# Gating projection's second half on 512-column matmuls in pairs of banks, and squares added ahead of three sums over partitions

## The chip, the cores and the metric

The kernel runs on one core of one Trainium2 chip. The metric is the device time of one execution in microseconds (us). The engines are named as in the profile: PE (TensorE, with PEld for its weight loads), DVE (VectorE), ACT (ScalarE), POOL (GpSimd), and SP, which here only issues DMAs.

## What is computed

The program is two residual blocks over 256 tokens of width 1024, one after the other, in fp32. Activations lie transposed on the chip: `x` is 128 partitions x 8 channel tiles x 256 tokens. What matters here, cut from the reference:

```python
def _spatial_gating_mixer(h, w_in, b_in, ln_g, ln_b, w_s, b_s, w_out):
    z = jax.nn.gelu(h @ w_in + b_in, approximate=False)
    u, v = jnp.split(z, 2, axis=-1)              # 2048 columns each
    v = _layernorm(v, ln_g, ln_b, LN_EPS)
    ...
    s = jnp.einsum('gij,bnjgc->bnigc', w_s, v) + b_s.T[None, None, :, :, None]
    y = u * s.reshape(bsz, seq, SGU_WIDTH)
    return y @ w_out

def _rmsnorm(x, g):
    y = xf * lax.rsqrt(jnp.mean(xf * xf, axis=-1, keepdims=True) + RMS_EPS)
    return (y * g.astype(jnp.float32)).astype(x.dtype)
```

The phases in order are a mixer, FFN 1, the gating mixer above, FFN 2, an RWKV mixer, FFN 3, and a last norm. Every norm needs the sum of the squares of a token over all 1024 channels, that is over 8 tiles and 128 partitions.

## The kernel before

Weights come in units of 128 x 2048 elements (1 MB) through a ring of four slots. For each unit SP loads `raw`, ACT rounds it to `w_high` (`high`, L685), DVE forms `w_low = raw - w_high` (`low`, L1264), and PE waits for the low part (`lo_done`). Activations are split in the same way, into `act_hi` and `act_lo`, which lie side by side in `act_parts`. A product is then hi x hi + hi x lo + lo x hi, accumulated in PSUM. Each engine's order is the order in which its own code is written; engines meet through semaphores.

There are two forms of that product. `split_matmul` (L2133 to L2135) issues three 256-column matmuls into one 256-column half of a bank; one unit (`project`) is 2 column tiles x 8 `k` x 3 matmuls in one bank. The FFNs use `wide` (L2496, L2497): one 512-column matmul takes `w_high` against both activation parts at once, so that the main term and the cross term land in the two halves of one bank, and a 256-column matmul adds `w_low` x `act_hi` to the second half. A unit then takes two banks, and the halves have to be added afterwards: ACT copies the second half to SBUF (`copy_half`, L897), DVE adds the first half from PSUM (`add_half`, L1584).

In the gating mixer (units 28 of the whole list onwards, `U_SGU`), eight units give `v` (banks 0 to 3), then eight units give `u`, one bank each, banks 0 and 1 in turn. For unit `c` of `u` the work is:

- PE: `project` after `u_raw >= c - 1` (the unit two before has left its bank); two `row_sums` ahead of `c` = 2, `spatial` ahead of `c` = 4 and 5. Before the first `accumulate` of the output projection, which writes banks 2 to 5, it waits for `v_raw >= 8`, the last use of banks 2 and 3.
- DVE: multiply the bank by the token scale `r2` (L1780, gives `u_raw`); from `c` = 1 on `low` of unit 11 + c; besides `normalise_values` at `c` = 1 (L1755), `row_sums` at 2 and 3 (L1713), two `final_norm` at 2 to 5 (L1718), and `gate(0)`, `gate(1)` at 5 and 6 (L1766, L1771, then L1775 after ACT's `gated_high`, L975).
- ACT: two Gelus after `u_raw` (L980), `high` of unit 12 + c, at `c` = 1 a table load and a small rsqrt (L697, L689, L691), at 5 and 6 `gated_high`.

Sums over partitions are fp32 matmuls against a matrix of ones. In the FFNs POOL first adds the eight tiles of squares (`fold_squares`, L637, L639) and PE needs one matmul (L2547). At the entry of the RWKV mixer PE takes eight (`input_sums`, L2650), tiles 0 to 5 in one row directly after FFN 2, tiles 6 and 7 after a first group of `small_products`. Ahead of the last norm it takes eight again (L3053), directly behind the last FFN matmul; ACT makes these squares (L1247 to L1251) as the tiles of `x` are finished, and DVE meanwhile finishes the last two tiles (`last_taken`, L1646 and L1648), multiplies `x` by the norm's weights (L2121) and at the end by the token scale (L2126). In `mlp(2)` ACT squares all of `x` for FFN 3's own norm in one instruction (L881) between the `high` of its third unit and that of its fourth.

## Time and profile before

| | |
|---|---|
| median of 3 runs | 1044.14 us (1043.94 to 1044.15) |
| profiled execution, its own time | 1044.1 us |
| its span, first to last instruction | 1042.2 us |
| PE busy | 1025.3 us, 98% |
| DVE busy | 824.7 us, 79% |
| ACT busy | 558.9 us, 54% |
| POOL busy | 54.9 us, 5% |
| mean granted TensorE clock | 0.998 |

In a row of the timeline the first number is the start in us from the start of the span, the second the duration. A matmul's record includes the time in which it fills and drains, so records overlap: the pace of PE is the distance from start to start, not the duration. The span is 1.9 us shorter than the execution's own time; that part lies around the program.

### The profile page before, as it was taken

Reading aid. Unit: us, or ns where it says so; the run is one execution under the profiler, and the core shown is the slowest. Engines: PE = TensorE matmul, PEld = TensorE weight load, DVE = VectorE, ACT = ScalarE, POOL = GpSimd, SP = SyncE. Lnnn points to the kernel's source line nnn. Section 1 sums busy time; section 2 is a strip of 40 time slices with the busy share of each in tenths; the row PEclk is TensorE's granted clock in tenths of the full one; section 3 lists DMA queues with packets and bytes.
Section 4 is the critical chain, followed back from the end, with each engine's and each line's share of the span. In section 5 each row is a group of like instructions: output and inputs, shape, how many; then the busy total and the mean of one; then the engine's idle time right before and its main releaser. Section 6 shows DMA issues by size and latency. Waiting matters only on the chain.

```text
span 1042.2 us, 17910 instructions
## 1 busy us (share of the span) xinstructions
PE 1025.3 (98%) x7496; PEld 927.8 (89%) x7496; DVE 824.7 (79%) x1167; ACT 558.9 (54%) x685; POOL 54.9 (5%) x48
## 2 busy tenths in 40 slices
PE   7999999999999999999999999999999999999997
PEld 7999988888887899998888889999898998888886
DVE  6989688677787787678878878899978668877775
ACT  6847554544456464355446447797543255444441
POOL 0004030000000000020000000042000001000000
PEclk9999999999999999999999999999999999999999
DMA  9722566566846745555656555424100156656621
GB/s 291 230 82 82 162 202 202 162 204 187 311 147 184 221 162 205 160 168 166 199 174 222 166 199 162 142 86 150 50 3 2 52 185 210 202 163 201 191 93 41
DMA packets 155937, 167.24 MB, mean 160 GB/s; under 512 B 5840, under 2 KB 148816, under 8 KB 155472
## 3 DMA queue, kind: packets, MB, share of 16 engines
q1 hardware_dynamic: 154672, 165.92, 50.2%
q8 instruction: 60, 0.98, 0.4%
q10 hardware_dynamic: 1184, 0.17, 0.2%
q14 instruction: 21, 0.17, 0.0%
HBM read 165.03 MB, written 1.05 MB: 159 GB/s over the span
## 4 chain that ended last, share of the span: by engine, by line
PE 83%; DVE 11%; ACT 3%; issue 2%; SPq 1%; DMA 1%; DVEq 0%; ACTq 0%
PE banks L2496 32%; PE banks L2497 16%; PE banks L2133 8%; PE banks L2135 8%; PE banks L2134 8%; DVE sb_w_low L1264 2%; DVE sb_arena L1966 1%; DVE sb_state L1963 1%; DMA sb_raw<-in_w_in 1%; ACT sb_w_high L685 1%; PE banks L2754 1%; PE banks L2621 1%; SPq L550 1%; PE banks L2865 0%; DVE sb_arena L1432 0%
## 5 line engine op out<-in xcount | busy, mean ns | idle before, releaser
L1264 DVE TENSOR_TENSOR sb_w_low<-sb_raw,sb_w_high 128x2048 fp32r<-128x2048 f32 x148 | 341.3, 2310 | 33.1 <-ACT sb_w_high L685 33.1
L685 ACT ACTIVATE sb_w_high<-sb_raw 128x2048 fp32r<-128x2048 f32 x148 | 281.7, 1908 | 11.3 <-PE banks L2135 10.2
L2496 PE MATMUL banks<-sb_act_parts,sb_w_high 128*128 128x512 f32 x768 | 270.6, 394 | 0.4 <-DVE sb_act_parts L1529 0.4
L2497 PE MATMUL banks<-sb_act_parts,sb_w_low 128*128 128x256 f32 x768 | 214.5, 279 | 0.0
L897 ACT ACTIVATE sb_arena<-banks 128x512 f32<-128x512 f32 x93 | 55.5, 597 | 244.7 <-PE banks L2497 244.7
L2496 PEld LDWEIGHTS banks<-sb_act_parts,sb_w_high 128*128 128x128 f32 x768 | 143.9, 187 | 36.1 <-DVE sb_act_parts L1529 0.7
L2133 PE MATMUL banks<-sb_act_parts,sb_w_low 128*128 128x256 f32 x584 | 169.3, 290 | 0.7 <-DVE sb_arena L1839 0.7
L2135 PE MATMUL banks<-sb_act_parts,sb_w_high 128*128 128x256 f32 x584 | 165.0, 282 | 0.0
L2134 PE MATMUL banks<-sb_act_parts,sb_w_high 128*128 128x256 f32 x584 | 163.9, 281 | 0.0
L2497 PEld LDWEIGHTS banks<-sb_act_parts,sb_w_low 128*128 128x128 f32 x768 | 144.0, 188 | 0.0
L2496 PE MATMUL banks<-sb_hidden_slots,sb_w_high 128*128 128x512 f32 x360 | 131.5, 397 | 0.6 <-DVE sb_hidden_slot L1597 0.6
L1584 DVE TENSOR_TENSOR sb_arena<-sb_arena,banks 128x512 f32<-128x512 f32 x93 | 63.7, 685 | 86.1 <-ACT sb_arena L897 86.0
L2496 PE MATMUL banks<-sb_hidden_slot,sb_w_high 128*128 128x512 f32 x360 | 130.2, 394 | 0.0
L2133 PEld LDWEIGHTS banks<-sb_act_parts,sb_w_low 128*128 128x128 f32 x584 | 109.9, 188 | 2.5 <-DVE sb_arena L1839 0.9
L2134 PEld LDWEIGHTS banks<-sb_act_parts,sb_w_high 128*128 128x128 f32 x584 | 110.8, 190 | 0.5 <-issue 0.2
L2135 PEld LDWEIGHTS banks<-sb_act_parts,sb_w_high 128*128 128x128 f32 x584 | 109.3, 187 | 0.0
L2497 PE MATMUL banks<-sb_hidden_slots,sb_w_low 128*128 128x256 f32 x360 | 101.1, 281 | 0.0
L2497 PE MATMUL banks<-sb_hidden_slot,sb_w_low 128*128 128x256 f32 x360 | 100.8, 280 | 0.0
L2496 PEld LDWEIGHTS banks<-sb_hidden_slots,sb_w_high 128*128 128x128 f32 x360 | 67.7, 188 | 17.5 <-DVE sb_w_low L1264 0.9
L2496 PEld LDWEIGHTS banks<-sb_hidden_slot,sb_w_high 128*128 128x128 f32 x360 | 67.5, 187 | 16.1
L2497 PEld LDWEIGHTS banks<-sb_hidden_slots,sb_w_low 128*128 128x128 f32 x360 | 67.6, 188 | 0.1
L2497 PEld LDWEIGHTS banks<-sb_hidden_slot,sb_w_low 128*128 128x128 f32 x360 | 67.5, 188 | 0.0
(473 smaller groups left out, 1544.2 us busy)
## 6 DMA issues: line engine op xcount, KB each, us to landing
sb_raw<-in_ffn_w SPq DMA_DIRECT2D x64, 1024.0 KB, 5.4
sb_raw<-in_w_up SPq DMA_DIRECT2D x16, 1024.0 KB, 5.5
sb_raw<-in_w_down SPq DMA_DIRECT2D x16, 1024.0 KB, 5.1
sb_raw<-in_sgu_w_in SPq DMA_DIRECT2D x16, 1024.0 KB, 5.6
sb_raw<-in_rwkv_w_rkv SPq DMA_DIRECT2D x12, 1024.0 KB, 5.2
sb_raw<-in_w_in SPq DMA_DIRECT2D x8, 1024.0 KB, 9.7
sb_raw<-in_sgu_w_out SPq DMA_DIRECT2D x8, 1024.0 KB, 4.9
sb_raw<-in_w_out SPq DMA_DIRECT2D x4, 1024.0 KB, 5.2
```

Of the source, the lines that this page charges most:

```text
L550: sp.dma_start(half_of(raw[j], t), w_in_v[:, :, c * 256 + t * P:c * 256 + t * P + P])\
L685: nc.scalar.activation(whi[s][:], raw[s][:], ACT.Copy).then_inc(hi_done, 1)
L897: nc.scalar.activation(dst, halves_at(FFN_BANK(m))[:, :, 1, :], ACT.Copy).then_inc(half_copied, 1)
L1264: nc.vector.tensor_tensor(wlo[s][:], raw[s][:], f32(whi[s][:]), ALU.subtract).then_inc(lo_done, 1)
L1584: nc.vector.tensor_tensor(t, t, halves_at(FFN_BANK(m))[:, :, 0, :], ALU.add).then_inc(unit_taken, 1)
L1963: base.add(nc.vector.tensor_tensor(tmp, RW.LB[:, j + 1:, j:j + 1].broadcast_to(shape), RW.WB[:, j:j + 1, 0:j + 1].broadcast_to(shape), ALU ...
L1966: base.add(nc.vector.tensor_tensor(RW.WB[:, j + 1:, 0:j + 1], RW.WB[:, j + 1:, 0:j + 1], tmp, ALU.add))
L2133: nc.tensor.matmul(dst, l_lo, r_hi, start=start, stop=False, **kw)
L2134: nc.tensor.matmul(dst, l_hi, r_lo, start=False, stop=False, **kw)
L2135: return nc.tensor.matmul(dst, l_hi, r_hi, start=False, stop=stop, **kw)
L2496: nc.tensor.matmul(two(dst), l_hi, parts, start=start, stop=False, skip_group_check=True)
L2497: return nc.tensor.matmul(dst[:, T:2 * T], l_lo, parts[:, 0, :], start=False, stop=stop, skip_group_check=True)
```

## The change

The eight `u` units of the gating mixer are issued with `wide`, into two banks each (0, 1 and 2, 3 in turn). ACT copies the second halves, DVE adds the first ones and then multiplies by `r2` in SBUF. PE now waits for the DVE addition (`u_added`), also ahead of the first `accumulate`. At the RWKV entry POOL adds the squares of tiles 0 to 3, so that PE takes one matmul for them. Ahead of the last norm POOL adds tiles 0 to 3 to two, DVE adds tiles 4 and 5 to those and both to one, in the middle of `last_taken`, and PE takes three matmuls. In FFN 3 the large square on ACT moves behind `high` of the fourth unit and the first `copy_half`.

```diff
@@ block.gpsimd, on["rwkv"] @@
+            pool.wait_ge(sq_done, SQ["rwkv"] + 2)
+            chain.add(pool.tensor_tensor(RW.sq[:, 0:2, :], RW.sq[:, 0:2, :], RW.sq[:, 2:4, :], ALU.add))
+            chain.settle()
+            pool.tensor_tensor(RW.sq[:, 0, :], RW.sq[:, 0, :], RW.sq[:, 1, :], ALU.add).then_inc(sq_paired, 1)
@@ block.gpsimd, on["end"] @@
             fold_squares(2)
+            pool.wait_ge(sq_done, SQ["final"] + 2)
+            pool.tensor_tensor(FB.sq[:, 0:2, :], FB.sq[:, 0:2, :], FB.sq[:, 2:4, :], ALU.add).then_inc(sq_paired, 1)
@@ block.scalar, mlp @@
-            nc.scalar.activation(FB.sq[:], x[:], ACT.Square).then_inc(sq_done, 1)
+            if j < 2:
+                nc.scalar.activation(FB.sq[:], x[:], ACT.Square).then_inc(sq_done, 1)
             high(u0 + 3)
...
                 copy_half(m)
+                if j == 2 and m == 0:
+                    nc.scalar.activation(FB.sq[:], x[:], ACT.Square).then_inc(sq_done, 1)
@@ block.scalar, gating, for c in range(8) @@
+                act.wait_ge(w_used, U_SGU + 8 + c + 1)
+                nc.scalar.activation(SG.U[:, 2 * c:2 * c + 2, :], halves_at(2 * (c % 2))[:, :, 1, :], ACT.Copy)\
+                    .then_inc(u_half, 1)
                 act.wait_ge(u_raw, c + 1)
@@ block.vector, mlp @@
+            def gather_squares():
+                dve.wait_ge(sq_paired, 2)
+                dve.wait_ge(sq_done, SQ["final"] + 3)
+                chain.add(nc.vector.tensor_tensor(FB.sq[:, 0:2, :], FB.sq[:, 0:2, :], FB.sq[:, 4:6, :], ALU.add))
+                chain.settle()
+                nc.vector.tensor_tensor(FB.sq[:, 0, :], FB.sq[:, 0, :], FB.sq[:, 1, :], ALU.add).then_inc(sq_gathered, 1)
...
                     if i:
+                        if j == 2:
+                            gather_squares()
                         dve.wait_ge(w_used, u0 + len(FFN_ORDER))
@@ block.vector, gating, for c in range(8) @@
-                dve.wait_ge(w_used, U_SGU + 8 + c + 1)
-                nc.vector.tensor_tensor(SG.U[:, 2 * c:2 * c + 2, :], two(bank[c % 2][:]), over(r2, 2), ALU.mult)\
-                    .then_inc(u_raw, 1)
+                us = SG.U[:, 2 * c:2 * c + 2, :]
+                dve.wait_ge(u_half, c + 1)
+                nc.vector.tensor_tensor(us, us, halves_at(2 * (c % 2))[:, :, 0, :], ALU.add).then_inc(u_added, 1)
+                dve.wait_ge(u_added, c + 1)
+                nc.vector.tensor_tensor(us, us, over(r2, 2), ALU.mult).then_inc(u_raw, 1)
@@ block.tensor @@
+        def project_wide(u, b):
...
+            for t in range(2):
+                for k in range(KT):
+                    cs = slice(t * P, t * P + P)
+                    ins = wide(bank[b + t], h[:, k, cs], l[:, k, cs], act_parts[:, :, k, :], start=k == 0,
+                               stop=k == KT - 1)
+            ins.then_inc(w_used, 1)
@@ gating, for c in range(8) @@
                 if c >= 2:
-                    pe.wait_ge(u_raw, c - 1)
+                    pe.wait_ge(u_added, c - 1)
                 else:
-                    pe.wait_ge(v_raw, 6)
-                project(U_SGU + 8 + c, c % 2)
-            pe.wait_ge(v_raw, 8)
+                    pe.wait_ge(v_raw, 6 + 2 * c)
+                project_wide(U_SGU + 8 + c, 2 * (c % 2))
+            pe.wait_ge(u_added, 8)
             pe.wait_ge(t_done, 4)
@@ input_sums @@
-                pe.wait_ge(sq_done, SQ["rwkv"] + c + 1)
-                for k in (2 * c, 2 * c + 1):
+                if c == 0:
+                    pe.wait_ge(sq_paired, 1)
+                else:
+                    pe.wait_ge(sq_done, SQ["rwkv"] + c + 1)
+                for k in (2 * c, 2 * c + 1) if c else (0,):
@@ on["end"] @@
-            for k in range(KT):
-                pe.wait_ge(sq_done, SQ["final"] + (k // 2 + 1 if k < 6 else k - 2))
-                ins = nc.tensor.matmul(bank[6][:, 0:T], ones, FB.sq[:, k, :], start=k == 0, stop=k == KT - 1)
+            pe.wait_ge(sq_gathered, 1)
+            nc.tensor.matmul(bank[6][:, 0:T], ones, FB.sq[:, 0, :], start=True, stop=False)
+            for k in (6, 7):
+                pe.wait_ge(sq_done, SQ["final"] + k - 2)
+                ins = nc.tensor.matmul(bank[6][:, 0:T], ones, FB.sq[:, k, :], start=False, stop=k == KT - 1)
```

ACT, end of the gating mixer's `u` loop, before: the Gelus and `high` of `c` = 5, `gated_high(0)`, then `c` = 6 with `gated_high(1)`, then `c` = 7. L685 is `high`, L975 `gated_high`, L980 a Gelu; in brackets the semaphores waited for.

```order
L980 ACTIVATE sb_arena<-sb_arena,sb_vectors 128x256
L685 ACTIVATE sb_w_high<-sb_raw 128x2048 [waits unit_used,unit_landed0]
L975 ACTIVATE sb_hidden_high<-sb_arena 128x512 [waits gated]
L980 ACTIVATE sb_arena<-sb_arena,sb_vectors 128x256 [waits u_in]
L980 ACTIVATE sb_arena<-sb_arena,sb_vectors 128x256
L685 ACTIVATE sb_w_high<-sb_raw 128x2048 [waits unit_used,unit_landed1]
```

The same place with the change, from `c` = 6 on: L692 is `high`, L985 `gated_high`, L989 the new copy of the second halves, L993 a Gelu.

```order
L989 ACTIVATE sb_arena<-banks 128x512 [waits unit_used]
L993 ACTIVATE sb_arena<-sb_arena,sb_vectors 128x256 [waits u_in]
L993 ACTIVATE sb_arena<-sb_arena,sb_vectors 128x256
L692 ACTIVATE sb_w_high<-sb_raw 128x2048 [waits unit_used,unit_landed0]
L985 ACTIVATE sb_hidden_high<-sb_arena 128x512 [waits gated]
L989 ACTIVATE sb_arena<-banks 128x512 [waits unit_used]
L993 ACTIVATE sb_arena<-sb_arena,sb_vectors 128x256 [waits u_in]
L993 ACTIVATE sb_arena<-sb_arena,sb_vectors 128x256
```

The copy of the last unit stands behind `high`, and behind a `gated_high` that waits for DVE.

DVE at the same place with the change, from `gate(0)` on: L1789 to L1798 are `gate`, L1804 is the new addition, L1806 the multiplication, L1277 is `low`.

```order
L1798 TENSOR_TENSOR sb_hidden_low<-sb_arena,sb_hidden_high 128x512 [waits gated,hidden_hi]
L1804 TENSOR_TENSOR sb_arena<-sb_arena,banks 128x512 [waits u_half_copied]
L1806 TENSOR_TENSOR sb_arena<-sb_arena 128x512 [waits u_halves_added]
L1277 TENSOR_TENSOR sb_w_low<-sb_raw,sb_w_high 128x2048 [waits unit_high]
L1789 SCALAR_TENSOR_TENSOR sb_arena<-banks,sb_vectors,sb_arena 128x256 [waits spatial_in_psum]
L1789 SCALAR_TENSOR_TENSOR sb_arena<-banks,sb_vectors,sb_arena 128x256
L1794 TENSOR_TENSOR sb_arena<-sb_arena 128x512 [waits u_activated,dve_chain]
L1798 TENSOR_TENSOR sb_hidden_low<-sb_arena,sb_hidden_high 128x512 [waits gated,hidden_hi]
L1804 TENSOR_TENSOR sb_arena<-sb_arena,banks 128x512 [waits u_half_copied]
L1806 TENSOR_TENSOR sb_arena<-sb_arena 128x512 [waits u_halves_added]
```

Each unit has two DVE instructions where it had one; the addition of the last unit stands behind `low` and all of `gate(1)`.

PE with the change, the last `wide` pair of the last `u` unit and the first matmuls of `accumulate`:

```order
L2179 MATMUL banks<-sb_act_parts,sb_w_high 128x512
L2180 MATMUL banks<-sb_act_parts,sb_w_low 128x256
L2158 MATMUL banks<-sb_hidden_high,sb_w_low 128x256 [waits hidden_lo,unit_low,spatial_shift,u_halves_added]
L2159 MATMUL banks<-sb_hidden_low,sb_w_high 128x256
L2160 MATMUL banks<-sb_hidden_high,sb_w_high 128x256
```

Nothing stands between the last unit and the matmul that waits for `u_halves_added`; before, that matmul waited for `v_in` in its place.

## Rows read from the trace of the kernel before

**Rows 1.** Page: the chain that ended last, share of the span by engine.

```profile
PE 83%; DVE 11%; ACT 3%; issue 2%; SPq 1%; DMA 1%; DVEq 0%; ACTq 0%
```

**Rows 2.** Timeline of PE: split unit, first accumulate, wide unit (start, duration, engine, line).

```profile
369.24 0.28 PE L2133 MATMUL banks<-sb_act_parts,sb_w_low 128*128 128x256 f32 x1
...
374.99 0.29 PE L2133 MATMUL banks<-sb_act_parts,sb_w_low 128*128 128x256 f32 x1
...
405.21 0.28 PE L2133 MATMUL banks<-sb_hidden_high,sb_w_low 128*128 128x256 f32 x1
...
899.84 0.39 PE L2496 MATMUL banks<-sb_act_parts,sb_w_high 128*128 128x512 f32 x1
...
905.44 0.39 PE L2496 MATMUL banks<-sb_act_parts,sb_w_high 128*128 128x512 f32 x1
```

**Rows 3.** Timeline of DVE in the gating mixer.

```profile
365.63 0.67 DVE L1780 TENSOR_TENSOR sb_arena<-banks,sb_arena 128x512 f32<-128x512 f32 x1
...
373.54 2.60 DVE L1755 TENSOR_SCALAR sb_arena<-sb_arena 128x2048 f32<-128x2048 f32 x2 [2.17 <-ACT sb_arena L691]
376.06 0.68 DVE L1780 TENSOR_TENSOR sb_arena<-banks,sb_arena 128x512 f32<-128x512 f32 x1
376.65 2.28 DVE L1264 TENSOR_TENSOR sb_w_low<-sb_raw,sb_w_high 128x2048 fp32r<-128x2048 f32 x1
...
379.89 0.87 DVE L1718 SCALAR_TENSOR_TENSOR sb_x<-sb_x,sb_vectors,sb_arena 128x256 f32<-128x256 f32 x2
380.68 0.68 DVE L1780 TENSOR_TENSOR sb_arena<-banks,sb_arena 128x512 f32<-128x512 f32 x1
...
397.49 0.87 DVE L1766 SCALAR_TENSOR_TENSOR sb_arena<-banks,sb_vectors,sb_arena 128x256 f32<-128x256 f32 x2
...
400.39 0.68 DVE L1780 TENSOR_TENSOR sb_arena<-banks,sb_arena 128x512 f32<-128x512 f32 x1
```

**Rows 4.** Timeline of ACT in the gating mixer.

```profile
367.15 1.90 ACT L685 ACTIVATE sb_w_high<-sb_raw 128x2048 fp32r<-128x2048 f32 x1
368.95 0.90 ACT L980 ACTIVATE sb_arena<-sb_arena,sb_vectors 128x256 f32<-128x256 f32 x2
369.75 1.91 ACT L685 ACTIVATE sb_w_high<-sb_raw 128x2048 fp32r<-128x2048 f32 x1
```

**Rows 5.** Timeline of ACT, then of DVE, in FFN 3: copy, addition, multiplication.

```profile
882.35 0.60 ACT L897 ACTIVATE sb_arena<-banks 128x512 f32<-128x512 f32 x1 [6.06 <-PE banks L2497]
...
882.98 0.69 DVE L1584 TENSOR_TENSOR sb_arena<-sb_arena,banks 128x512 f32<-128x512 f32 x1 [1.64 <-ACT sb_arena L897]
883.70 0.69 DVE L1604 TENSOR_TENSOR sb_arena<-sb_arena 128x512 f32<-128x512 f32 x1
```

**Rows 6.** Windows of PE at the end: stretch, length, busy, granted clock, DMA.

```profile
1038.00:1039.00 1.00, 0.00 (x0) 0.55 0.81 259
```

**Rows 7.** Timeline of PE at the start; the chain at the end.

```profile
5.48 5.40 PE L2242 MATMUL banks<-sb_x,sb_ones 128*128 128x256 f32 x12 [5.48 <-DMA sb_x<-in_x_t]
10.38 0.62 PE L2221 MATMUL banks<-sb_act_parts,sb_w_high 128*128 128x256 f32 x1
...
1032.15 3.47 PE banks L3053 x16
```

**Rows 8.** Timelines around FFN 3's start: POOL, DVE, PE.

```profile
857.57 6.42 POOL L637 TENSOR_TENSOR sb_arena<-sb_arena 128x1024 f32<-128x1024 f32 x2 [116.62 <-ACT sb_arena L881]
...
859.33 3.50 DVE L1264 TENSOR_TENSOR sb_w_low<-sb_raw,sb_w_high 128x2048 fp32r<-128x2048 f32 x1 [0.92 <-ACT sb_w_high L685]
...
874.33 0.48 PE L2496 MATMUL banks<-sb_hidden_slots,sb_w_high 128*128 128x512 f32 x1 [0.56 <-DVE sb_hidden_slot L1597]
```

**Rows 9.** Timeline of DVE, then ACT, at the end.

```profile
1032.19 0.42 DVE L1646 TENSOR_TENSOR sb_arena<-banks,sb_arena 128x256 f32<-128x256 f32 x1 [1.88 <-PE banks L2135]
...
1036.67 2.56 DVE L2126 TENSOR_TENSOR sb_x<-sb_x,sb_arena 128x256 f32<-128x256 f32 x5 [1.49 <-ACT sb_arena L691]
...
1033.11 0.42 ACT L1251 ACTIVATE sb_arena<-sb_x 128x256 f32<-128x256 f32 x1 [2.35 <-DVE sb_x L1648]
```

More of the change, by code:

```diff
@@ L254, in build_on @@
     out_used = sem("output_activation_used")
-    sq_folded = sem("squares_folded")
+    sq_folded, sq_paired, sq_gathered = sem("squares_folded"), sem("squares_paired"), sem("squares_gathered")
     wo_done = sem("mixer_outputs_used")
@@ L365, in build_on @@
         "gating_norms", "gating_squares_folded", "gating_scales_in_psum", "u_in"))
+    u_half, u_added = sem("u_half_copied"), sem("u_halves_added")
     FFN_A = [A_FFN1, A_FFN2, A_FFN3]
@@ L2150, in project, with wide @@
             return last
+        def wide(dst, l_hi, l_lo, parts, start, stop):
+            nc.tensor.matmul(two(dst), l_hi, parts, start=start, stop=False, skip_group_check=True)
+            return nc.tensor.matmul(dst[:, T:2 * T], l_lo, parts[:, 0, :], start=False, stop=stop,
+                                    skip_group_check=True)
+        def project_wide(u, b):
+            s = u % RING
+            h, l = (w[s][:, :].rearrange("p (k n) -> p k n", k=KT) for w in (whi, wlo))
+            pe.wait_ge(lo_done, u + 1)
+            for t in range(2):
[4 more added lines that the diff above has]
+            ins.then_inc(w_used, 1)
         def quarter(u, b, n):
@@ L2492, in mlp @@
             u0, h0, a0 = FFN_U[j], FFN_H[j], FFN_A[j]
-            def wide(dst, l_hi, l_lo, parts, start, stop):
-                nc.tensor.matmul(two(dst), l_hi, parts, start=start, stop=False, skip_group_check=True)
-                return nc.tensor.matmul(dst[:, T:2 * T], l_lo, parts[:, 0, :], start=False, stop=stop,
-                                        skip_group_check=True)
             def begin(m):
@@ L2664, in _ @@
             input_sums(0)
-            input_sums(1)
             input_sums(2)
```

## Prediction

> **What bounds the kernel now.** I read the page's chain first: PE is 83% of it [rows 1], so an edit pays if it takes time from PE where PE waits for nobody, and costs if it makes PE wait. Then the timelines of PE, DVE and ACT at the four places that the change touches. In the gating mixer's `u` units PE runs without a gap and DVE and ACT wait for it: the Gelus and `gate` have idle time in front of them. At the RWKV entry PE goes straight from FFN 2 into the ones-matmuls. At FFN 3's start it waits 0.56 us for the third hidden slot [rows 8]. At the end it runs eight ones-matmuls back to back, while DVE idles 1.49 us ahead of the last multiplication [rows 9].
>
> **The `u` units on PE.** A split unit is 16 groups of three 256-column matmuls: 369.24 to 374.99, 5.75 us. A wide unit is 16 pairs: 899.84 to 905.44, 5.60 us [rows 2]. Eight units save 1.2 us. A 256-column matmul is thus paced at 0.120 us, and a 512-column one at 0.350 - 0.120 = 0.230 us. The Trainium skill, TensorE: Matmul & The Clock Gate (Part 1, "Wait — 56ns, not 53.3ns?"), adds about 2.5 ns of fixed cost to columns over 2.4 GHz, which would leave 2.5 ns per pair, 0.3 us for all 128; the trace shows 9 ns, so the rows decide. As it turns out below, neither matters.
>
> **What DVE and ACT get in return.** Per unit ACT has a copy more and DVE an instruction more (add in PSUM, then multiply). PE's next-but-one unit waits for the addition; so does the first `accumulate`, for the last unit's, since it writes into banks 2 and 3. Behind each wait on ACT stands `high`, behind each on DVE `low`. I therefore lay the loop out again from the first unit's addition, which starts at 365.63 as the multiplication did [rows 3]. Prices: copy to addition 0.63, addition to multiplication 0.72 [rows 5], and I take 0.72 again for multiplication to Gelu; Gelus to `high` 0.80, `high` to the next ACT instruction 1.80 [rows 4]; multiplication to the next DVE instruction 0.6, `low` 2.2, `low` with row sums 3.24, `final_norm` 0.79, all of `gate` 2.90 [rows 3].
>
> - Addition 1: ACT does Gelu and `high` of unit 0 before the copy of unit 1. 365.63 + 0.72 + 0.72 + 0.80 + 1.80 + 0.63 = 370.30.
> - Addition 2: Gelu, `high`, then table load, rsqrt and `normalise_values`. From that `high` to `normalise_values` it is 373.54 - 369.75 = 3.79 [rows 3, 4], and that takes 2.52. 370.30 + 0.72 + 0.72 + 0.80 + 3.79 + 2.52 = 378.85.
> - Additions 3 and 4, bound by DVE: 0.72 + 0.60 + 3.24 + 0.79 = 5.35 each, 384.20 and 389.55.
> - Addition 5, bound by ACT: 4.67, 394.22.
> - Addition 6, bound by DVE with `gate(0)`: 0.72 + 0.60 + 2.20 + 0.79 + 2.90 = 7.21, 401.43.
> - Addition 7: behind `low` and `gate(1)`, 6.42, starts 407.85 and ends 408.54. ACT's copy is no earlier than 0.1 us before that, since it stands behind `gated_high(1)`.
>
> Until unit 7 every addition is ready before PE asks (the closest is addition 2: it ends at 379.5, and unit 4 starts at 380.7, four units of 5.60 and one `spatial` of some 0.9 ahead of 404.0). PE is done with unit 7 at 405.21 - 1.2 = 404.0 [rows 2], then has nothing: the next matmul waits for addition 7. With 0.2 us to restart, `accumulate` starts at 408.74 in place of 405.21: **+3.5 us**, and the 1.2 us saved on PE are only a longer wait. Behind it everything is PE's again (DVE's hidden parts are ready), so it stays lost. Bounds: the layout adds some thirty handoffs of 0.6 to 3 us; with 0.03 us on each it moves by 0.9 us either way.
>
> **The clock.** PE would idle 4.7 us. The trace of before has no such gap in its middle; its longest in the rows is 0.56 us. It has two ends. At the end PE stops at 1032.15 + 3.47 = 1035.62 [rows 7], and the granted clock of 1038 to 1039 is 0.55 of full [rows 6]: it fell to the lower level (1.2 GHz) at 1038.1, 2.5 us after the last matmul. At the start six ones-matmuls take 10.38 - 5.48 = 4.90 us; at the end eight take 3.47, so six 2.60 [rows 7]: PE came out of idleness at half pace, and lost 2.3 us until it was at 2.4 GHz. A gap of 4.7 us is longer than 2.5, so I count **+2.3 us**; the bounds are 0 (it does not fall) and some 3. TensorE: Matmul & The Clock Gate in the Trainium skill (Part 1, "Seeing it yourself") shows a run in which the clock fell only 5.2 us after the last matmul; by that delay it would not fall here, and the time would be that of the second case below. The row of this kernel speaks against it.
>
> **RWKV entry.** Three ones-matmuls fewer, at 3.47 / 8 = 0.434 us [rows 7]: -1.30 us. POOL's two adds start when the second pair of squares is done, behind the last but two `down` unit's part of `x` and so a whole FFN unit (5.60 us) ahead of PE; POOL took 6.42 us for 1536 elements [rows 8], 3.2 for these 768, so they are ready. But they hold DVE: while POOL folded, a `low` took 3.50 us instead of 2.28 [rows 8], 1.22 us more. DVE is on the way to the last squares here, and they have about 1 us of slack once PE is earlier. I take **-1.2**, between -1.3 and -0.1.
>
> **FFN 3's start.** `high` of the fourth unit no longer stands behind the square, so its `low` starts at once, 0.92 us earlier [rows 8]; but POOL's fold moves some 2.3 us later (`high`'s 1.80 and a copy of 0.5) and now blocks DVE in several smaller steps. PE's wait there is 0.56 us [rows 8], which is the most that can be won. **-0.3**, between -0.6 and +0.3.
>
> **The end.** PE's last square is ready at 1033.11 + 0.42 = 1033.53 [rows 9]; one matmul behind it, 0.43 plus 0.4 to start and drain (an estimate), and then the 1.05 us that lie between 1035.62 and 1036.67 [rows 7, 9]: 1035.4. POOL's add holds DVE up for about 1 us (at most 1.22) at the tiles before the last, and the two gathering adds take 0.72 + 0.42 (as the copied tile's) on DVE: 2.1 us, of which the 1.88 us that DVE idled ahead of the last tile [rows 9] swallow all but 0.2. So 1035.6 in place of 1036.67: **-1.0**. The most is DVE's idle 1.49, the least 0.6.
>
> Sum: +3.5 + 2.3 - 1.2 - 0.3 - 1.0 = +3.3. The profiled execution took 1044.1 us, as the median does (1044.14), so 1047.4 us.
>
> **The rivals.**
> 1. The wait comes, but the clock stays up: 1044.1 + 3.5 - 2.5 = 1045.1. For it: no gap of this length is seen in the middle of the trace, and a single fall is all the evidence. Against: 2.5 us is well under 4.7. 23%.
> 2. On the other side, faster: additions keep up with PE and `accumulate` does not wait. That needs addition 7 to end before 404.0, so the loop of 42 us to be 4.6 us shorter, as if ACT's copies and DVE's second instruction cost nothing. Then the 1.2 us of the wide units count: 1044.1 - 1.2 - 2.5 = 1040.4. Against: DVE's sum of instructions per unit leaves it no idleness from unit 2 on. For: DVE and ACT waited for PE in before. From a wait of 1.3 us on (3.4 less than mine) the gain is gone. 8%.
> 3. POOL's adds hold DVE so long that the squares are late at both places, and neither sum gains: 1047.4 + 2.2 = 1049.6. For: 3.50 against 2.28 [rows 8]. Against: about 1 us of slack at the one, DVE's 1.88 of idleness at the other. 7%.
>
> **Numbers.** Forecast 62%, with 1046.2 to 1048.5 as its own range (the layout's 0.9 us, the clock's 1.7 to 3). To hold 8 in 10 the range takes in rival 1 down to 1044.2, and part of rival 3: 1044.0 to 1049.0. What a measurement can tell here is 0.2%, 2.1 us, so "same" is 1042.0 to 1046.2: rival 1 and the lower edge of the forecast, 27%. Slower: the rest of the forecast and rival 3, 65%. Faster: rival 2, 8%.
>
> **What would show it.** In the profile after: one idle stretch of PE of 4 to 5 us ahead of the first `accumulate`, released by the DVE addition of the last unit; ACT's last copy behind `gated_high(1)`; wide units at 5.60 us; a granted clock under 1.00 around 408 us, and matmul pace doubled for some us after it; at the RWKV entry one ones-matmul less than two in place of four for the first tiles; at the end the last multiplication 1.0 us nearer to the last FFN matmul. The prediction is wrong if that wait is under 3 us, or if the clock stays at 1.00 through it, or if the waits are spread over the earlier units.

## The result and the profile after

The changed kernel takes 1046.31 us (median of 20 runs, 1045.22 to 1048.58) where the kernel before, on the same chip, takes 1044.35 (20 runs, 1043.94 to 1047.25). The ratio of the runs is 1.0021, with a 95% interval of 1.0014 to 1.0027: some 2 us slower, on the very bound of 0.2% that the prediction set between "same" and "slower". A second sample of ten runs gave 1046.20 beside 1044.20, ratio 1.0025 (1.0014 to 1.0035). 1047.4 was forecast, with 1044.0 to 1049.0.

| | before | after, first profile | after, second profile |
|---|---|---|---|
| profiled execution, us | 1044.1 | 1048.58 | 1046.17 |
| span, us | 1042.2 | 1046.8 | 1044.4 |
| mean granted clock | 0.998 | 0.996 | 0.995 |
| first `u` unit's result taken by DVE, us | 365.63 | 367.48 | 365.59 |
| first `accumulate` matmul, us | 405.21 | 410.46 | 408.56 |
| idle PE just before it, us | none | 4.46 | 4.45 |
| last multiplication of the final norm starts, us | 1036.67 | 1041.27 | 1038.87 |

The first profile fell on the slowest of its 20 executions. It was already 1.85 us late at the first `u` unit [rows 3], ahead of everything that the change touches. So a second profile was taken, which starts as the kernel before did.

The page's chain by engine, after, where [rows 1] had PE 83% and DVE 11%:

```profile
PE 77%; DVE 14%; ACT 4%; issue 2%; DMA 1%; SPq 1%; DVEq 0%; ACTq 0%
```

The waits of PE in the profile after (what it waited for: us in all, times, longest):

```profile
PE banks L2158 <- DVE sb_arena L1804: 4.5, 1, 4.5
PE banks L2329 <- DVE sb_arena L1398: 1.5, 1, 1.5
...
PE banks L3094 <- ACT sb_arena L1264: 0.3, 1, 0.3
```

The first is new and is the one forecast: `accumulate` (L2158) waits for DVE's addition (L1804). The second lies in the first mixer and comes with the late start: the second profile does not have it. The third is the last square, at the end. The wait of 0.56 us for a hidden slot [rows 8] is no longer in the list.

Six of DVE's eight additions in the second profile (start, duration, idle time before and what ended it):

```profile
365.59 0.67 DVE L1804 TENSOR_TENSOR sb_arena<-sb_arena,banks 128x512 f32<-128x512 f32 x1
...
370.24 0.69 DVE L1804 TENSOR_TENSOR sb_arena<-sb_arena,banks 128x512 f32<-128x512 f32 x1 [1.64 <-ACT sb_arena L989]
...
378.81 0.68 DVE L1804 TENSOR_TENSOR sb_arena<-sb_arena,banks 128x512 f32<-128x512 f32 x1
...
394.18 0.69 DVE L1804 TENSOR_TENSOR sb_arena<-sb_arena,banks 128x512 f32<-128x512 f32 x1 [0.27 <-ACT sb_arena L989]
401.40 0.68 DVE L1804 TENSOR_TENSOR sb_arena<-sb_arena,banks 128x512 f32<-128x512 f32 x1
...
407.82 0.68 DVE L1804 TENSOR_TENSOR sb_arena<-sb_arena,banks 128x512 f32<-128x512 f32 x1
```

Behind the first, the layout said 370.30, 378.85, 394.22, 401.43 and 407.85. Each is off by less than 0.07 us, and only two of the shown ones wait for ACT's copy; the others stand behind DVE's own work. In the first profile the last copy is where it was put, right behind `gated_high(1)` (L985) on ACT:

```profile
408.45 0.63 ACT L985 ACTIVATE sb_hidden_high<-sb_arena 128x512 fp32r<-128x512 f32 x1 [1.00 <-DVE sb_arena L1794]
408.99 0.58 ACT L989 ACTIVATE sb_arena<-banks 128x512 f32<-128x512 f32 x1
```

PE around the gap, first profile, the end of unit 7 and the start of `accumulate`:

```profile
405.72 0.28 PE L2180 MATMUL banks<-sb_act_parts,sb_w_low 128*128 128x256 f32 x1
410.46 0.58 PE L2158 MATMUL banks<-sb_hidden_high,sb_w_low 128*128 128x256 f32 x1 [4.46 <-DVE sb_arena L1804]
410.84 0.41 PE L2159 MATMUL banks<-sb_hidden_low,sb_w_high 128*128 128x256 f32 x1
411.06 0.41 PE L2160 MATMUL banks<-sb_hidden_high,sb_w_high 128*128 128x256 f32 x1
...
416.39 0.34 PE L2158 MATMUL banks<-sb_hidden_high,sb_w_low 128*128 128x256 f32 x1
416.57 0.28 PE L2159 MATMUL banks<-sb_hidden_low,sb_w_high 128*128 128x256 f32 x1
416.69 0.28 PE L2160 MATMUL banks<-sb_hidden_high,sb_w_high 128*128 128x256 f32 x1
```

And the windows of the same stretch (stretch, length, busy time and count of PE, PEld, DVE, ACT and POOL, granted clock, DMA share, GB/s):

```profile
406.00:409.00 3.00, 0.00 (x0) 0.00 (x0) 2.39 (x4) 2.00 (x3) 0.00 (x0) 1.00 0.26 52
409.00:410.00 1.00, 0.00 (x0) 0.00 (x0) 0.88 (x2) 0.57 (x2) 0.00 (x0) 0.84 0.97 397
410.00:411.00 1.00, 0.54 (x2) 0.54 (x3) 0.96 (x2) 0.00 (x0) 0.00 (x0) 0.50 1.03 426
411.00:416.00 5.00, 5.00 (x26) 5.00 (x25) 4.42 (x3) 3.99 (x4) 0.00 (x0) 0.50 0.32 95
```

A mean of 0.84 over 409 to 410 is 0.68 us at 1.00 and the rest at 0.50. So the clock fell to 1.2 GHz at 409.7, 3.7 us after the end of the last matmul. PE then starts a matmul every 0.213 us instead of 0.120 until 416.4: 27 steps take 5.93 us. In the run with the gap filled (below), where the clock stays up, the same 27 steps take 3.34 (408.68 to 412.02). That is 2.6 us lost.

The RWKV entry after, three ones-matmuls, then two, and what follows each (a ones-matmul is two records here):

```profile
645.23 1.46 PE L2690 MATMUL banks<-sb_over_act,sb_ones 128*128 128x256 f32 x6
...
646.34 0.47 PE L2158 MATMUL banks<-sb_mixer_input_high,sb_lora_low 128*128 128x256 f32 x1
...
647.95 1.05 PE L2690 MATMUL banks<-sb_over_act,sb_ones 128*128 128x256 f32 x4
...
648.65 0.47 PE L2158 MATMUL banks<-sb_mixer_input_high,sb_lora_low 128*128 128x256 f32 x1
```

Before, the entry runs from 637.16 and work goes on behind the last pair at 641.87:

```profile
637.16 2.75 PE L2650 MATMUL banks<-sb_over_act,sb_ones 128*128 128x256 f32 x12
...
641.87 0.47 PE L2133 MATMUL banks<-sb_mixer_input_high,sb_lora_low 128*128 128x256 f32 x1
```

4.71 us became 3.42: 1.29 won. FFN 3's start after, from the ones-matmul to the first matmul on a hidden slot, and POOL's fold, to be held against [rows 8]:

```profile
866.69 4.71 POOL L638 TENSOR_TENSOR sb_arena<-sb_arena 128x1024 f32<-128x1024 f32 x2 [118.96 <-ACT sb_arena L916]
...
868.08 2.17 DVE L1603 SCALAR_TENSOR_TENSOR sb_arena<-sb_arena 128x512 f32<-128x512 f32 x1
...
880.00 0.59 PE L2584 MATMUL banks<-sb_arena,sb_ones 128*128 128x256 f32 x2
880.35 0.47 PE L2179 MATMUL banks<-sb_hidden_slots,sb_w_high 128*128 128x512 f32 x1
```

The step from the ones-matmul to the next is 0.35 us. Before, those two stood 1.16 us apart (873.17 and 874.33):

```profile
873.17 0.59 PE L2547 MATMUL banks<-sb_arena,sb_ones 128*128 128x256 f32 x2
```

So 0.81 us was won, not the 0.56 that the record of idle time shows. POOL's fold still holds DVE up (2.17 us for an instruction that takes 0.69 elsewhere), but earlier than anybody waits. The end, after, where [rows 9] had 1032.19, 1033.11 and 1036.67:

```profile
1037.62 0.42 DVE L1656 TENSOR_TENSOR sb_arena<-sb_arena 128x256 f32<-128x256 f32 x1
1038.12 0.42 DVE L1669 TENSOR_TENSOR sb_arena<-banks,sb_arena 128x256 f32<-128x256 f32 x1
1039.03 0.42 ACT L1264 ACTIVATE sb_arena<-sb_x 128x256 f32<-128x256 f32 x1 [1.66 <-DVE sb_x L1671]
1039.50 0.70 PE L3094 MATMUL banks<-sb_arena,sb_ones 128*128 128x256 f32 x2 [0.28 <-ACT sb_arena L1264]
1041.27 2.56 DVE L2151 TENSOR_TENSOR sb_x<-sb_x,sb_arena 128x256 f32<-128x256 f32 x5 [0.16 <-ACT sb_arena L698]
```

From the last tile's product (L1669) to the last multiplication (L2151) it is 3.15 us; it was 4.48. That is 1.33 won, and the gathering additions (L1656) end just in time for L1669, which is not delayed.

The whole sum for the first profile: late start +1.85, wait +3.40 (410.46 - 405.21 - 1.85), the rest of what the RWKV entry is late by +2.82 (645.23 - 637.16 - 1.85 - 3.40; 2.6 of it the half pace, 0.2 not placed), RWKV -1.29, FFN 3 -0.81, end -1.33. Together +4.64, against 4.60 at the last multiplication and 4.48 in the times.

### The profile page after: what moved, and what is told of

Read it like the earlier page. It is cut to its first block, busy times and chain, and to the rows that moved or that the text cites. A ratio compares the mean times of both kernels' runs of the same rounds, so it can differ in the third digit from the quotient of the medians.

```text
span 1046.8 us, 17644 instructions
## 1 busy us (share of the span) xinstructions
PE 1024.0 (98%) x7352; PEld 920.3 (88%) x7352; DVE 833.3 (80%) x1177; ACT 563.1 (54%) x693; POOL 58.3 (6%) x51
## 3 DMA queue, kind: packets, MB, share of 16 engines
HBM read 165.03 MB, written 1.05 MB: 159 GB/s over the span
## 4 chain that ended last, share of the span: by engine, by line
PE 77%; DVE 14%; ACT 4%; issue 2%; DMA 1%; SPq 1%; DVEq 0%; ACTq 0%
PE banks L2179 33%; PE banks L2180 17%; PE banks L2158 6%; PE banks L2160 6%; PE banks L2159 6%; DVE sb_w_low L1277 3%; ACT sb_w_high L692 1%; DVE sb_arena L1991 1%; DVE sb_state L1988 1%; DMA sb_raw<-in_w_in 1%; PE banks L2793 1%; SPq L551 1%; PE banks L2658 1%; DVE sb_arena L1804 0%; DVE sb_arena L1736 0%
## 5 line engine op out<-in xcount | busy, mean ns | idle before, releaser
L1277 DVE TENSOR_TENSOR sb_w_low<-sb_raw,sb_w_high 128x2048 fp32r<-128x2048 f32 x148 | 340.1, 2302 | 35.2 <-ACT sb_w_high L692 35.2
L2179 PE MATMUL banks<-sb_act_parts,sb_w_high 128*128 128x512 f32 x896 | 316.2, 395 | 0.4 <-DVE sb_act_parts L1542 0.4
L692 ACT ACTIVATE sb_w_high<-sb_raw 128x2048 fp32r<-128x2048 f32 x148 | 281.6, 1908 | 16.5 <-PE banks L2160 13.8
L2179 PEld LDWEIGHTS banks<-sb_act_parts,sb_w_high 128*128 128x128 f32 x896 | 168.0, 187 | 42.0 <-DVE sb_act_parts L1542 0.7
L2158 PE MATMUL banks<-sb_act_parts,sb_w_low 128*128 128x256 f32 x456 | 132.6, 291 | 0.7 <-DVE sb_arena L1864 0.7
L2160 PE MATMUL banks<-sb_act_parts,sb_w_high 128*128 128x256 f32 x456 | 128.8, 282 | 0.0
L2159 PE MATMUL banks<-sb_act_parts,sb_w_high 128*128 128x256 f32 x456 | 128.1, 281 | 0.0
L2158 PEld LDWEIGHTS banks<-sb_act_parts,sb_w_low 128*128 128x128 f32 x456 | 85.9, 188 | 2.2 <-DVE sb_arena L1864 0.9
L2159 PEld LDWEIGHTS banks<-sb_act_parts,sb_w_high 128*128 128x128 f32 x456 | 86.4, 190 | 0.2
L2160 PEld LDWEIGHTS banks<-sb_act_parts,sb_w_high 128*128 128x128 f32 x456 | 85.4, 187 | 0.0
```

The source lines that it names most:

```text
L692: nc.scalar.activation(whi[s][:], raw[s][:], ACT.Copy).then_inc(hi_done, 1)
L1277: nc.vector.tensor_tensor(wlo[s][:], raw[s][:], f32(whi[s][:]), ALU.subtract).then_inc(lo_done, 1)
L2158: nc.tensor.matmul(dst, l_lo, r_hi, start=start, stop=False, **kw)
L2159: nc.tensor.matmul(dst, l_hi, r_lo, start=False, stop=False, **kw)
L2160: return nc.tensor.matmul(dst, l_hi, r_hi, start=False, stop=stop, **kw)
L2179: nc.tensor.matmul(two(dst), l_hi, parts, start=start, stop=False, skip_group_check=True)
```

## The experiments

The theory is that three edits of the squares win 3.4 us, and that the gating edit loses more than that: a wait for the eighth addition and, behind it, PE at half clock. A first rival is that the clock has nothing to do with it. A second is that DVE is full, so that any cure for the one wait makes another.

**The gating half undone.** Units split again, one multiplication on DVE, no copy on ACT:

```
-                project_wide(U_SGU + 8 + c, 2 * (c % 2))
-            pe.wait_ge(u_added, 8)
+                project(U_SGU + 8 + c, c % 2)
+            pe.wait_ge(v_raw, 8)
```

> The changed kernel with the gating half as it was before: only the squares' edits and FFN 3's moved square are left. By my reading of the changed kernel's trace the RWKV entry gave 1.15 us (with what follows up to mixer 4's end 1.25), FFN 3's start 0.85 and the end 1.33: 3.4 us in all, so 1044.35 - 3.4 = 1040.9 us. By the prediction's own terms (1.2, 0.3, 1.0) it would be 1041.85. Rival: most of what the three places show was won back from delays that only exist because the gating part comes late; then under 2 us, 1042.4 or more. The runs should lie as close together as the kernel before's (most within 0.5 us), since no long gap of PE is left in the middle.

1040.63 us (5 runs, 1040.28 to 1041.07) against 1044.24: ratio 0.9965 (0.9953 to 0.9978). The squares win 3.6 us by themselves by the medians, and not the 2.5 of the prediction's terms. In the profile the way from the first `u` result to the last multiplication is 667.61 us instead of 671.04: 3.43 won, as the three places say (1.29 + 0.81 + 1.33).

**The gating edit alone.** The changed kernel without anything of the squares; of the RWKV entry, for instance:

```
-                for k in (2 * c, 2 * c + 1) if c else (0,):
+                for k in (2 * c, 2 * c + 1):
```

> The kernel before with the gating edit alone (wide units, ACT's copy, DVE's addition, accumulate behind the eighth addition). Theory: the wait costs 3.4 us net of the 1.2 us saved, and the fallen clock 2.75 as in the one profile, so 1044.35 + 6.15 = 1050.5 us. Rival: in most runs the clock falls later or for shorter than in the profiled one (which was the slowest of its 20), and the clock costs 1 to 2.5 us: 1048.8 to 1050.2. Rival, clock never the matter: 1047.75. Runs spread over 2 to 3 us as the changed kernel's do.

1049.78 us (5 runs, 1049.58 to 1051.66), ratio 1.0059 (1.0046 to 1.0071): 5.5 us slower. The three squares' edits and this one add up: -3.6 + 5.5 = +1.9 against the measured +2.0. Its windows (columns as above):

```profile
405.00:407.00 2.00, 0.00 (x0) 0.00 (x0) 1.86 (x4) 1.00 (x2) 0.00 (x0) 1.00 0.34 43
407.00:408.00 1.00, 0.00 (x0) 0.00 (x0) 0.41 (x1) 1.00 (x2) 0.00 (x0) 0.60 0.80 283
408.00:414.00 6.00, 5.07 (x23) 5.07 (x24) 5.39 (x5) 4.04 (x5) 0.00 (x0) 0.50 0.42 148
```

Here the clock fell at 407.2, and PE was back at full pace at 414.0, 5.1 us after it started again at 408.93. Its first 40 steps behind the wait take 7.12 us, those of the run with the gap filled 4.90. That costs 2.2 us, and not the expected 2.75: here the rival came, with its 1 to 2.5 us and its 1048.8 to 1050.2.

**The gap filled.** PE is kept busy until the addition is ready, the wait itself stays:

```
+            pe.wait_ge(u_added, 7)
+            for _ in range(19):
+                nc.tensor.matmul(bank[0][:, 0:P], ones, ones, start=True, stop=True)
             pe.wait_ge(u_added, 8)
```

> The changed kernel with 19 matmuls of the ones matrix on itself (128 columns, some 0.22 us each, 4.2 us in all) into a bank that is free, put between the last u unit and the wait for the eighth addition. The wait's end stays where it is (accumulate still starts 3.4 us later than before), PE is merely busy until then. Theory: the granted clock stays at 1.00 through 420 us, no half pace, and the 2.75 us are gone: 1044.35 + 3.4 - 3.4 = 1044.35 us, between 1043.9 and 1044.7, and the runs close together. Rival: the slow matmuls behind the gap, or the spread of the runs, have another cause than the clock: 1046.3 as the changed kernel.

The profiled execution took 1043.76 us and shows what was to be shown. `accumulate` still starts late, at 408.68, and the clock stays up:

```profile
404.00:409.00 5.00, 4.78 (x42) 4.59 (x41) 4.24 (x7) 2.79 (x3) 0.00 (x0) 1.00 0.54 180
409.00:416.00 7.00, 7.00 (x61) 7.00 (x60) 4.85 (x3) 5.20 (x5) 0.00 (x0) 1.00 0.58 184
```

61 matmuls start in the 7 us behind the wait, at full pace. Against the second profile of the changed kernel (1046.17, with the same start) that is 2.4 us for nothing but useless matmuls. The rival that leaves the clock out is gone. The median of 11 runs is 1045.30, though, and the runs do not lie close together as I had expected: five take 1043.76 to 1044.22 and six 1045.30 to 1046.30. The clock is not what parts them. The mean granted clock of all eleven is 0.998 or 0.999, where the 30 runs of the changed kernel, in its two samples, have 0.992 to 0.997. The likely cause is the start, which is taken up below; of the six slower runs none was profiled.

**The changed kernel once more**, for a second profile.

> The changed kernel once more, for a second profile and a second sample of its times. Theory: what makes its runs lie 1045.2 to 1048.6 apart is, first, the start (in some executions ACT waits some 1.5 us longer for a transfer of the first mixer's weights, as in the profiled one, where everything was 1.85 us late at the first u unit) and, second, how long the low clock lasts behind the gap (loss 2.2 us in the run with the gating edit alone, 2.6 in the changed kernel's profile). So this profile, if its time is below 1046.5, shows the first addition at 365.6 to 366, the same 4.5 us of idle PE ahead of accumulate, a granted clock of 0.50 behind it, and a median near 1046. Rival: a run of under 1046 us is one in which the clock did not fall in the gap.

1046.20 us (10 runs, 1045.56 to 1050.91). The profiled execution, 1046.17, starts on time (365.59), has the same 4.45 us of idle PE, and the clock fell all the same, here 2.8 us after the end of the last matmul:

```profile
404.00:406.00 2.00, 0.11 (x1) 0.00 (x0) 1.97 (x4) 1.55 (x1) 0.00 (x0) 1.00 0.00 0
406.00:407.00 1.00, 0.00 (x0) 0.00 (x0) 0.52 (x1) 0.45 (x1) 0.00 (x0) 0.93 0.88 152
407.00:408.00 1.00, 0.00 (x0) 0.00 (x0) 0.79 (x2) 0.67 (x2) 0.00 (x0) 0.50 0.87 352
408.00:413.00 5.00, 4.45 (x21) 4.45 (x22) 4.39 (x4) 3.72 (x4) 0.00 (x0) 0.50 0.37 125
```

So a run near the median is not one in which the clock stayed up; it is one with the early start. Two of the ten runs, 1049.24 and 1050.91, lie beyond what the late start explains; their mean granted clocks, 0.994 and 0.992, are lower than in the others, and no profile shows why. The late start of the first profile can be seen on ACT. This is a 1 MB part of the first mixer's weights, first in the first profile and then in the second one:

```profile
23.47 1.92 ACT L692 ACTIVATE sb_w_high<-sb_raw 128x2048 fp32r<-128x2048 f32 x1 [2.57 <-DMA sb_raw<-in_w_in]
```

```profile
21.98 1.92 ACT L692 ACTIVATE sb_w_high<-sb_raw 128x2048 fp32r<-128x2048 f32 x1 [0.85 <-DMA sb_raw<-in_w_in]
```

ACT waits 2.57 us for it instead of 0.85, and everything up to the first `u` unit is 1.6 to 2.1 us late. Four of the profiles taken here show this (the first of the changed kernel and those with six wide units, with the upper banks first and with the shortened gap). By the times the kernel before has such executions too (4 of its 20 runs beside the changed kernel are over 1045.5), but its one profile is not of such a run.

**A shorter gap.** Fewer ones-matmuls than in the filled one:

```
-            for _ in range(19):
+            for _ in range(6):
```

> The changed kernel with 6 ones-matmuls (some 1.3 us) in place of 19 between the last u unit and the wait for the eighth addition: PE then stands still for 3.2 us instead of 4.5. Theory: in the two profiles the clock fell 2.9 and 3.9 us after the last matmul, and 2.5 us at the end of the kernel before, so at 3.2 us it falls in some executions and not in others: between 1043.9 (it never falls) and 1046 (always), with single runs at either. Rival: the fall needs a standstill longer than 3.2 us, all runs as the filled gap's (1043.8 to 1044.2, or 1.5 more with the late start).

1045.63 us (11 runs, 1043.85 to 1048.40). The profiled execution (the slowest, with a late start of 1.9 us) shows a gap of 3.12 us and a fall at 409.5, 2.2 us after the last ones-matmul:

```profile
409.00:410.00 1.00, 0.00 (x0) 0.00 (x0) 0.84 (x2) 0.61 (x2) 0.00 (x0) 0.77 0.91 377
410.00:416.00 6.00, 5.50 (x25) 5.50 (x26) 5.39 (x4) 3.99 (x4) 0.00 (x0) 0.50 0.47 153
```

Two runs, 1043.85 and 1044.10, are as fast as the fast ones with the gap filled, in which it did not fall. The mean granted clock parts the eleven runs in two: six have 0.998, as with the gap filled, and take 1043.85 to 1046.32, and five have 0.996 or 0.997, as in the changed kernel, and take 1045.54 to 1048.40. That fits "in some executions and not in others", but only one of the eleven was profiled, so for the others it is inferred from their mean clock. (The expectation counts from the start of the last matmul; from its end the two profiles have 2.7 and 3.7 us.)

**The wait shortened from the other side.** The first `accumulate` writes banks 4 and 5 first, which nobody holds:

```
+                n = (i_n + 4) % KT if first and u == U_SGO else i_n
+                if first and u == U_SGO and i_n == 4:
+                    pe.wait_ge(u_added, 8)
```

> The changed kernel; the first accumulate writes banks 4 and 5 first (24 matmuls, 2.9 us) and waits for the eighth addition only before banks 2 and 3. Theory 1 (the wait is for banks 2 and 3 alone, and the clock falls only when PE stands still for longer than some 3.6 us, as it did 3.7 and 3.5 us after the last matmul in the two profiles): 4.6 us of standing become 1.7, the clock stays at 1.00, and the time is 1044.24 - 3.6 + (1.7 - 1.2) = 1041.2 us. Rival, DVE as the bound: DVE is full from unit 2 on, so what the first accumulate no longer waits, the third one waits for its hidden low half (1.34 us in the run with six wide units, though that had 1.4 us less of DVE's work): 1042.5 to 1044. Rival, the clock falls at any stop: 1044.

1043.11 us (11 runs, 1042.71 to 1044.84), ratio 0.9987 (0.9978 to 0.9996). It beats both kernels, but does not reach the 1041.2 of theory 1. (The 3.5 us in the expectation is a misreading: in the run with the gating edit alone the clock fell 2.7 us after the last matmul.) The waits say why:

```profile
PE banks L2158 <- DVE sb_arena L1804: 1.6, 1, 1.6
...
PE banks L2158 <- DVE sb_hidden_low L1798: 1.3, 1, 1.3
```

The gap at the first `accumulate` is 1.6 us, and the clock stayed at 1.00 from 408 to 411. But now the third `accumulate` waits 1.3 us for `gate(2)`'s low part. DVE and ACT hand weights and gates over in one order, and are late by the time that the additions and copies have cost them. In the changed kernel there is no such wait; the 4.5 us before the first `accumulate` had covered it. This is the rival, DVE as the bound, with its 1042.5 to 1044.

**Six units wide, two split** (6 and 7 in banks 0 and 1, without copy and addition):

```
-                project_wide(U_SGU + 8 + c, 2 * (c % 2))
-            pe.wait_ge(u_added, 8)
+                if c < 6:
+                    project_wide(U_SGU + 8 + c, 2 * (c % 2))
+                else:
+                    project(U_SGU + 8 + c, c % 2)
+            pe.wait_ge(u_added, 6)
```

> The changed kernel, but units 6 and 7 as before (split, banks 0 and 1, no copy on ACT and one multiplication on DVE); units 0 to 5 are wide. The first accumulate then waits for addition 5 (about 394 us) alone and starts when PE is done, 6 x 0.15 = 0.9 us earlier than in the kernel before; nothing idles, the clock stays up. 1044.35 - 0.9 - 3.4 = 1040.05 us, faster than both kernels. Rival: with DVE full from unit 2 on, unit 7's multiplication and gate(1) come too late for the second accumulate, and a wait of 1 to 2 us stands there: 1041 to 1042, no better than without the gating edit.

1042.79 us (11 runs, 1041.38 to 1043.51), ratio 0.9982 (0.9973 to 0.9991). No wait is left at the first `accumulate`, but the same one as above at the third:

```profile
421.18 0.38 PE L2163 MATMUL banks<-sb_hidden_high,sb_w_low 128*128 128x256 f32 x1 [1.34 <-DVE sb_hidden_low L1799]
```

The rival's 1041 to 1042 came, with seven of eleven runs that look like late starts on top (1042.7 and more; the other four take 1041.4 to 1041.7). It is worse than no wide unit at all (1040.63).

**Five wide, three split** (5, 6 and 7 in banks 2, 0 and 1):

```
+                if c < 5:
+                    project_wide(U_SGU + 8 + c, 2 * (c % 2))
+                else:
+                    project(U_SGU + 8 + c, {5: 2, 6: 0, 7: 1}[c])
+            pe.wait_ge(u_raw, 6)
```

> The changed kernel with units 0 to 4 wide and 5, 6 and 7 split as before (banks 2, 0 and 1). By the DVE-bound reading of the run with six wide units (the third accumulate waited 1.34 us for gate(2)), DVE has some 4.8 us of idle time from unit 4 on when all are split (1.85 and 2.97 us ahead of multiplications 4 and 5), and five additions and their lateness just fit in it; six do not. So 1040.63 - 5 x 0.15 = 1039.9 us, no wait over 0.5 us in accumulate. Rival: DVE's lateness does not depend on the last unit but on ACT's copies and high parts; then a wait of 1 us or more stands at the third accumulate again, and the time is 1041 or more.

1040.39 us (5 runs, 1040.06 to 1041.59), ratio 0.9962 (0.995 to 0.9975). There is no wait in the `u` units or in `accumulate`. DVE is just in time: the multiplication of unit 6 starts at 400.32, as in the kernel before (400.39, [rows 3]):

```profile
393.82 0.68 DVE L1811 TENSOR_TENSOR sb_arena<-banks,sb_arena 128x512 f32<-128x512 f32 x1
...
400.32 0.68 DVE L1811 TENSOR_TENSOR sb_arena<-banks,sb_arena 128x512 f32<-128x512 f32 x1
```

This is the fastest version tried, 3.99 us under the kernel before that ran beside it and some 6 under the changed one. By the medians it is not told apart from the one without wide units (1040.63), and it misses the expected 1039.9; they ran beside different samples. In the profile `accumulate` starts 38.81 us after the first `u` result instead of 39.58: the 0.75 us of the five wide units are won there. At the last multiplication 0.44 of it is left (667.17 us against 667.61). Where the rest went was not followed up.

**Five wide alone:** the same edit in the kernel before, without those of the squares.

> The kernel before with units 0 to 4 wide and 5 to 7 split, and none of the other edits. Theory: nothing waits in the u units, PE saves 5 x 0.15 = 0.75 us: 1043.5 us. Rival: the saving is below what pace suggests, as 1040.39 against 1040.63 hints (0.24 by the medians of five runs): 1044.1.

1043.88 us (11 runs, 1043.05 to 1045.28) against 1044.20, ratio 0.9998 (0.9989 to 1.0007). By the times it is inconclusive: 0.3 us by the medians, and the interval holds both theory and rival. The profile speaks for the theory: from the first `u` result it is 38.82 us to the first `accumulate` (39.58 before) and 670.28 to the last multiplication (671.04 before), 0.76 won at both.

**The three squares' edits one by one.** The RWKV entry alone, in the kernel before (with POOL's two additions):

```
-            input_sums(0)
-            input_sums(1)
-            input_sums(2)
+            input_sums(0)
+            input_sums(2)
```

> The kernel before with the RWKV entry's edit alone (POOL adds four squares to one, three ones-matmuls fewer). Theory: PE saves 3 x 0.43 = 1.3 us and gives 0.15 back at the last sums: 1044.24 - 1.2 = 1043.05 us. Rival, the lock of DVE by POOL costs as much as PE saves: 1044.2.

1043.05 us (11 runs) against 1044.38, ratio 0.9988 (0.9979 to 0.9996): 1.3 us. Entry and sums take 637.24 to 640.66, 3.42 us, as in the changed kernel.

The end alone (with POOL's and DVE's additions):

```
-            for k in range(KT):
+            for k in (6, 7):
```

> The kernel before with the end's edit alone (POOL's and DVE's additions of squares, three ones-matmuls in place of eight). Theory: the last multiplication comes 1.33 us earlier as in the changed kernel's trace: 1044.24 - 1.3 = 1042.9 us. By the prediction's term 1043.2. Rival: the transfers of the output, not the multiplications, set the end, and less than 0.5 us is won.

1043.43 us (11 runs) against 1044.38, ratio 0.9990 (0.9981 to 0.9999): 0.95 us by the medians, with five runs over 1044.2. In its profile the first `u` unit's result is taken at 365.92, 0.29 late, and the last multiplication starts at 1035.73 instead of 1036.67, so 1.23 was won there.

FFN 3's square moved, alone:

```
+            if j < 2:
                 nc.scalar.activation(FB.sq[:], x[:], ACT.Square).then_inc(sq_done, 1)
...
                 copy_half(m)
+                if j == 2 and m == 0:
+                    nc.scalar.activation(FB.sq[:], x[:], ACT.Square).then_inc(sq_done, 1)
```

> The kernel before with FFN 3's square moved behind the first copy, and nothing else. Theory: the whole step from the last ones-matmul to the first down matmul shrinks from 0.81 us to none: 1044.35 - 0.85 = 1043.5 us, and the wait for the hidden slot is gone from the profile. By the prediction's term 1044.05. Rival: the gain in the changed kernel came from FFN 3 beginning later against its weights' transfers; then nothing is won here, 1044.3.

1043.28 us (11 runs) against 1044.20; the interval of the ratio, 0.9985 to 1.0003, just holds 1. The profile settles it, the wait is gone and the two matmuls stand 0.35 us apart:

```profile
873.36 0.59 PE L2571 MATMUL banks<-sb_arena,sb_ones 128*128 128x256 f32 x2
873.71 0.47 PE L2166 MATMUL banks<-sb_hidden_slots,sb_w_high 128*128 128x512 f32 x1
```

One by one the three give 1.3 + 0.95 + 0.9 = 3.2 us, together 3.6. The difference is within what medians of five and eleven runs carry.

## Why the prediction was right, and where it was off

1. **The wait before `accumulate`.** Right, in place and size: the eighth addition (addition 7 in the prediction's count) at 407.85 forecast, 407.82 measured; +3.5 forecast, +3.4 measured. The 0.1 is the restart, 0.2 in the sum, which is not seen: PE starts at 408.56, 0.06 behind the addition's end. That PE's saving of 1.2 us would be swallowed was right too: the last matmul of unit 7 starts at 403.83, so that PE could have gone on at 403.95 (404.0 forecast), and nobody gained by it.
2. **The clock.** Right: it fell in all three profiles that have the whole gap. +2.3 forecast; the half pace cost 2.6, 2.2 and 2.2 us, and filling the gap won 2.4. Both steps to that term rested on one sample each, and there was luck in it. That the clock would fall came from the 2.5 us at the end of the kernel before. At the ends of the fourteen profiles here this delay is anything from 1.5 us (the run with six wide units) to 5.0 (FFN 3's square alone), and in two of them it is longer than the gap of 4.5. The 2.3 us came from the pace at the start of the kernel; the granted clock recorded there, from 5 to 11 us, is 1.00, so the trace does not show that the clock was what made that pace. The Trainium skill, TensorE: Matmul & The Clock Gate (Part 1, "Seeing it yourself"), shows a fall 5.2 us after the last matmul, by which a gap of 4.5 us would have cost nothing. In the gaps here it fell 3.7, 2.8, 2.7 and 2.2 us after, and the measurement decides. That rival (23%) came in no profile, and the mean granted clocks (at most 0.997 in the changed kernel's 30 runs, at least 0.998 in the eleven with the gap filled) give no sign of it in any other run with the whole gap; with the shortened gap six of eleven runs look like it.
3. **The RWKV entry.** -1.2 forecast, -1.29 in the profile and -1.3 alone. POOL's hold on DVE, for which 0.1 had been kept back, cost nothing. (For the first four tiles PE takes one ones-matmul in place of four; the prediction's last paragraph says this unclearly.)
4. **FFN 3's start.** Mis-sized, and outside its bounds: -0.3 forecast (-0.6 to +0.3), -0.81 measured. Two things in that term failed. "0.56 us, which is the most that can be won": a wait costs the distance between two starts, less what they need anyway (1.16 - 0.35), and the recorded idle time is shorter, since it begins only at the modelled end of the matmul. And POOL's later fold does hold DVE up (2.17 us for 0.69), but not where PE waits.
5. **The end.** -1.0 forecast, -1.33 measured, within its bounds. The 0.2 that the gathering additions were to cost was not paid: L1669 starts 0.32 us behind the start of the last FFN matmul, as its counterpart did before (0.31). POOL's addition did hold DVE up, by 0.9 us (1.58 for an instruction of 0.69 at 1034.54), about the 1 us of the term. The way from the last ones-matmul to the multiplication is 1.77 us (1039.50 to 1041.27), where the term had 0.43 + 0.4 + 1.05 = 1.88.
6. **The sum.** 3.4 + 2.2 - 1.3 - 0.8 - 1.3 = 2.2, so 1046.3 instead of 1047.4. The mechanism was as forecast; the miss of 1.1 us is mostly the two terms of the squares (0.5 and 0.3). The forecast's own range, 1046.2 to 1048.5, holds the median by 0.1 us, and the result lies on the bound between "slower" (65%) and "same" (27%): the interval of the ratio is 0.14 to 0.27%.
7. **Not foreseen.** The late start, 1.6 to 2.1 us in four of the fourteen profiles and, by the times, in part of the executions of most kernels here. It made the first profile 1.85 us slow, and makes medians of five to eleven runs uncertain by several tenths. The 20 runs of the changed kernel have nine over 1046.8, the 20 of the kernel before four over 1045.5, so some tenths of the measured 2.0 us may be its share; the median's place within the forecast's own range is partly luck.

Rival 2, faster because no wait comes, failed at its own condition: the eighth addition ended 4.4 us after PE was done. Rival 3, POOL making the squares late, had no part: both places gained at least what the terms said.

Left open is what decides between the early and the late landing of that transfer, and whether it comes more often with some of these kernels; no run was made for it.

## What to carry to other kernels

A cheaper form on PE that needs a copy on ACT and an addition on DVE for each result is paid by the engines that hand it over. Lay their instructions out one behind the other up to the point where PE needs the last result. Here five of eight units fit into the idle time that DVE had, and six or eight did not; the work that DVE no longer hides shows up at the next wait, wherever that is.

A stop of PE of several us can cost more than its length, since PE may come back at half clock: here 2.2 to 2.6 us on top of a gap of 4.5, and 2.6 on top of one of 3.1. If the stop cannot be removed, useless matmuls into a free bank keep the pace (2.4 us here). Take the price of a wait from start to start, not from the recorded idle time.
